# A streaming encoder step on one core: both out-projections as three rounded products

## What is computed

```python
def _mix_even(...):
    ...
    out = jnp.concatenate([o_a.reshape(bsz, L, A_W), o_b], axis=-1) @ w_out   # (L, 1024) @ (1024, 1024)

def _mix_odd(...):
    ...
    o = _rmsnorm(o.astype(h.dtype), norm_g) * jax.nn.silu(z.reshape(bsz, L, C_HEADS, C_HEAD_DIM))
    out = o.reshape(bsz, L, C_W) @ w_out

def _trunk(x, past, prm):
    for i in range(DEPTH):
        x = x + 0.5 * _swiglu(rmsnorm(x), ...)       # feed-forward, 1024 -> 2816 -> 1024
        x = x + mixed                                # even or odd mixer
        x = x + 0.5 * _swiglu(rmsnorm(x), ...)
```

## Time and profile before

| | |
|---|---|
| median of 3 runs | 1662.07 us (1659.82 to 1662.42) |
| profiled execution, its span | 1662.3 us |
| mean granted TensorE clock | 0.947 |
| TensorE busy | 1514.3 us (91%) |
| VectorE busy | 917.8 us (55%) |
| ScalarE busy | 587.6 us (35%) |
| GpSimd busy | 314.9 us (19%) |

### The profile page before, as it was taken

One profiled execution on the slowest core, in us unless ns is written; L12 is line 12 of the kernel. 1 busy time (PEld: TensorE's weight loads), 2 busy tenths in 40 slices (PEclk: granted clock), 3 DMA queues, 4 the chain that ended last, 5 costly groups with the idle time before them and its releaser, 6 DMA issues.

```text
span 1662.3 us, 25537 instructions
## 1 busy us (share of the span) xinstructions
PE 1514.3 (91%) x9878; PEld 1450.1 (87%) x9878; DVE 917.8 (55%) x1511; ACT 587.6 (35%) x881; POOL 314.9 (19%) x319
## 2 busy tenths in 40 slices
PE   7699998997779999999999998798869889999997
PEld 6699997996757999999999996698868776999997
DVE  3466554278542666555666543868864341666642
ACT  5233333446331433334333323354422321533321
POOL 2000023755004000021000123344334002000000
PEclk9899998999879999999999998798979899999999
DMA  8755850434103555952557722323300002455651
GB/s 203 151 151 151 214 149 25 127 107 149 38 1 94 140 147 150 232 135 76 153 151 191 195 69 55 94 84 102 106 22 1 1 19 85 126 147 147 169 162 40
DMA packets 323804, 189.52 MB, mean 114 GB/s; under 512 B 11146, under 2 KB 320902, under 8 KB 323734
## 3 DMA queue, kind: packets, MB, share of 16 engines
q1 hardware_dynamic: 321088, 181.95, 40.0%
q0 software_dynamic: 2064, 6.58, 1.9%
q10 hardware_dynamic: 588, 0.12, 0.0%
HBM read 183.22 MB, written 5.40 MB: 113 GB/s over the span
## 4 chain that ended last, share of the span: by engine, by line
PE 82%; DVE 10%; ACT 4%; issue 2%; DMA 1%; SPq 1%; POOL 0%; ACTq 0%; DVEq 0%; POOLq 0%
PE PS L560 18%; PE PS L561 18%; PE PS L562 18%; PE PS L610 4%; PE PS L626 3%; PE PS L627 3%; PE PS L628 3%; DVE RA L1920 2%; PE PS L1035 1%; PE PS L1018 1%; PE PS L1030 1%; DMA gu<-in_ffn_w_up 1%; DVE RB L1931 1%; PE PS L1108 1%; PE PS L972 1%
## 5 line engine op out<-in xcount | busy, mean ns | idle before, releaser
L560 PE MATMUL PS<-h_hi,w_parts 128*128 128x320 f32 x1408 | 440.9, 313 | 27.0 <-DVE w_parts L1596 15.5
L561 PE MATMUL PS<-h_lo,w_parts 128*128 128x320 f32 x1408 | 438.6, 311 | 0.0
L562 PE MATMUL PS<-h_hi,w_parts 128*128 128x320 f32 x1408 | 438.3, 311 | 0.0
L560 PEld LDWEIGHTS PS<-h_hi,w_parts 128*128 128x128 f32 x1408 | 267.6, 190 | 30.0 <-DVE w_parts L1596 16.0
L561 PEld LDWEIGHTS PS<-h_lo,w_parts 128*128 128x128 f32 x1408 | 267.6, 190 | 0.3
L562 PEld LDWEIGHTS PS<-h_hi,w_parts 128*128 128x128 f32 x1408 | 267.5, 190 | 0.0
L1169 ACT ACTIVATE w_parts<-gu 128x1024 fp32r<-128x1024 f32 x176 | 176.5, 1050 | 184.8 <-PE PS L562 154.3
L1596 DVE TENSOR_TENSOR w_parts<-gu,w_parts 128x1024 fp32r<-128x1024 f32 x176 | 207.9, 1223 | 44.0 <-ACT w_parts L1169 43.8
L560 PE MATMUL PS<-act_hi,w_parts 128*128 128x320 f32 x704 | 217.5, 309 | 0.0
L561 PE MATMUL PS<-act_lo,w_parts 128*128 128x320 f32 x704 | 217.5, 309 | 0.0
L562 PE MATMUL PS<-act_hi,w_parts 128*128 128x320 f32 x704 | 217.5, 309 | 0.0
(11 more groups left out here) (336 smaller groups left out, 2078.5 us busy)
## 6 DMA issues: line engine op xcount, KB each, us to landing
gu<-in_ffn_w_gate SPq DMA_DIRECT2D x88, 512.0 KB, 4.0
gu<-in_ffn_w_up SPq DMA_DIRECT2D x88, 512.0 KB, 5.2
dn<-in_ffn_w_down SPq DMA_DIRECT2D x32, 1408.0 KB, 7.0
gu<-in_od_w_in SPq DMA_DIRECT2D x32, 512.0 KB, 5.0
gu<-in_ev_w_in SPq DMA_DIRECT2D x26, 512.0 KB, 4.8
dn<-in_ev_w_out SPq DMA_DIRECT2D x4, 1024.0 KB, 5.5
dn<-in_od_w_out SPq DMA_DIRECT2D x4, 1024.0 KB, 5.4
bias_rows<-RB POOLq DMA_DIRECT2D x1, 1280.0 KB, 28.6
```

What stands on the lines that cost most here:

```text
L560: mm(out, w_hi, hi, start=first, stop=False)
L561: mm(out, w_hi, lo, start=False, stop=False)
L562: return mm(out, w_lo, hi, start=False, stop=last)
```

## The change

Both out-projections become three products. The output of the mixers is kept in two parts, ev_o_hi and ev_o_lo (od_o_hi, od_o_lo), the weights in tiles wo of two parts, 256 columns wide, two buffers for each layer.

- TensorE: project_out does 24 matmuls for each output tile instead of 8. It waits for the remainders of the weight tile (wo_lo) and the output's remainders. In the even layer it begins with k = 4 to 7 (the gated heads), which need o_lo 1, and waits for the attention heads (pv_evac) only at the fifth k.
- ScalarE: heads_high rounds the heads' output from PSUM, out_high the odd chunks', split_out the weights, in two halves of 128x1024. The rounding of tiles 2 and 3 waits for dn_done of the output tile that frees their buffer. In the even layer these stand behind the split of the next feed-forward's first weights; in the odd layer tile 2 stands ahead of it and tile 3 behind.
- VectorE: heads_low and out_low subtract instead of copying; split_out does the remainder of even tile 1 ahead of the feed-forward's split, and of tiles 2 and 3 ahead of residuals 2 and 4.
- GpSimd: the remainders of even tile 0 and of odd tiles 0 and 1.
- Loads: a slot of dn is free when its tile's remainder has been taken (wo_lo), not when the products are done. The csr rows and some semaphores move; their work is the same.

Hunks that only merge semaphores or move csr are left out here.

```diff
@@ -312,6 +312,13 @@
+        ev_o_hi = rounded("ev_o_hi", RB_at, KT, T)
+        ev_o_lo = rounded("ev_o_lo", RB_at + T_QB * T, KT, T)
+        ev_wo = (rounded("ev_wo0", RB_at + bd_at + 320, 2, 2048), rounded("ev_wo1", RA_at, 2, 2048))
+        od_o_hi = rounded("od_o_hi", RA_at + 2560, KT, T)
+        od_o_lo = rounded("od_o_lo", hT_at, KT, T)
+        od_wo = (rounded("od_wo0", RB_at + 5120, 2, 2048), rounded("od_wo1", RB_at + dm_at, 2, 2048))
+
         def product_bank(c):
@@ -418,7 +426,9 @@
                     return lo_done, halves_before(f, FT + n - DN_FFN[f] + 1)
-            return dn_done, n + 1
+            if n < DN_EV + 4:
+                return wo_lo, 2 * (n - DN_EV + 1)
+            return wo_lo, 8 + 2 * (n - DN_OD + 1)
@@ -600,15 +610,24 @@
-            def project_out(base_dn, base_x):
+            def project_out(base_dn, base_x, wo, lo_before, out_hi, out_lo, first):
                 for m in range(KT):
 ...
                     if m % 2 == 0:
-                        pe.wait_ge(dn_loaded[n % 2], 16 * (n // 2 + 1))
+                        pe.wait_ge(wo_lo, lo_before + 2 * (m // 2 + 1))
                     pe.wait_ge(x_upd, base_x + 1 + m)
-                    for k in range(KT):
-                        ins = mm(bank(4 + m % 2, T), dn[:, n % 2, k * 256 + (m % 2) * P:k * 256 + (m % 2) * P + P],
-                                 oT[:, k, :], start=(k == 0), stop=(k == KT - 1))
+                    out = bank(4 + m % 2, T)
+                    for i in range(KT):
+                        k = (first + i) % KT
+                        at = k * 256 + (m % 2) * P
+                        w_hi, w_lo = (wo[m // 2 % 2][:, part, at:at + P] for part in range(2))
+                        if m == 0 and base_dn == DN_EV and i == 0:
+                            pe.wait_ge(o_lo, 1)
+                        if m == 0 and base_dn == DN_EV and i == 4:
+                            pe.wait_ge(s["pv_evac"], NCH)
+                        mm(out, w_hi, out_hi[:, k, :], start=(i == 0), stop=False)
+                        mm(out, w_hi, out_lo[:, k, :], start=False, stop=False)
+                        ins = mm(out, w_lo, out_hi[:, k, :], start=False, stop=(i == KT - 1))
                     ins.then_inc((dn_half, dn_done)[m % 2], 1)
@@ -664,9 +683,9 @@
                 attention()
-                pe.wait_ge(s["ob_ready"], 4)
-                pe.wait_ge(s["pv_evac"], 5)
-                project_out(DN_EV, X_EV)
+                pe.wait_ge(s["l_done"], 8)
+                pe.wait_ge(s["pt_evac"], 8)
+                project_out(DN_EV, X_EV, ev_wo, 0, ev_o_hi, ev_o_lo, 4)
@@ -914,12 +933,12 @@
                 recurrence()
-                pe.wait_ge(o["og"], NCH)
-                project_out(DN_OD, X_OD)
+                pe.wait_ge(o_lo, 1 + NCH)
+                project_out(DN_OD, X_OD, od_wo, 8, od_o_hi, od_o_lo, 0)
 ...
-                pe.wait_ge(o["ab_in"], 48)
+                pe.wait_ge(small_in, 96)
                 for k in range(KT):
@@ -1293,6 +1312,16 @@
                     split_gate_up(2, 0, 0, 0)
+
+            def split_out(base_dn, m, wo):
+
+                n = base_dn + m
+                sc.wait_ge(dn_loaded[n % 2], 16 * (n // 2 + 1))
+                if m >= 2:
+                    sc.wait_ge(dn_done, n - 1)
+                for half in range(2):
+                    w = slice(half * 1024, (half + 1) * 1024)
+                    copy(wo[m % 2][:, 0, w], dn[:, n % 2, w]).then_inc(wo_hi, 1)
@@ -1401,23 +1430,41 @@
+                def heads_high(b):
+                    sc.wait_ge(s["pv_pe"], b + 1)
+                    for par in range(2):
+                        h = slice(par * A_D, (par + 1) * A_D)
+                        ins = copy(ev_o_hi[h, 0:4, b * CH:(b + 1) * CH],
+                                   bank((6, 7, 6, 7, 7)[b])[h, :].rearrange("p (a c) -> p a c", a=4)
+                                   [:, :, par * CH:(par + 1) * CH])
+                    ins.then_inc(o_hi, 1)
+
                 exps(0)
 ...
                 turned(1)
+                sc.wait_ge(out_sem, 16 * 8)
+                copy(ev_o_hi[:, 4:8, :], oT[:, 4:8, :]).then_inc(o_hi, 1)
                 turned(2)
+                heads_high(0)
+                heads_high(1)
                 exps(3)
                 turned(3)
+                heads_high(2)
                 exps_sample(0)
                 exps_sample(1)
+                heads_high(3)
                 turned_sample(0)
 ...
                 exps_sample(3)
+                split_out(DN_EV, 0, ev_wo)
                 turned_sample(2)
                 turned_sample(3)
+                heads_high(4)
+                split_out(DN_EV, 1, ev_wo)
@@ -1517,6 +1564,12 @@
+                def out_high(n_):
+
+                    w = slice(CHUNK_ORDER[n_] * CH, (CHUNK_ORDER[n_] + 1) * CH)
+                    sc.wait_ge(o["og"], n_ + 1)
+                    copy(od_o_hi[:, :, w], oT[:, :, w]).then_inc(o_hi, 1)
+
                 for n_, c in enumerate(CHUNK_ORDER):
@@ -1531,10 +1584,19 @@
                     act_(sqO, bank(2), ACT.Square).then_inc(o["osq"], 1)
+                    if n_ > 1:
+                        out_high(n_ - 2)
+                    if n_ == 2:
+                        sc.wait_ge(o["zt"], 2)
+                        split_out(DN_OD, 0, od_wo)
+                    if n_ == 3:
+                        split_out(DN_OD, 1, od_wo)
+                out_high(NCH - 2)
                 root_out(NCH - 1)
 ...
                 copy(csr[0:6, 2048:3072], PS[0:6, 3072:4096]).then_inc(o["cs_evac"], 1)
+                out_high(NCH - 1)
@@ -1549,6 +1611,8 @@
             split_gate_up(1, 0, 0, 0)
+            split_out(DN_EV, 2, ev_wo)
+            split_out(DN_EV, 3, ev_wo)
             ffn(1, C_FFN + 8, X_FFN[1])
@@ -1556,7 +1620,9 @@
             odd()
+            split_out(DN_OD, 2, od_wo)
             split_gate_up(3, 0, 0, 0)
+            split_out(DN_OD, 3, od_wo)
             ffn(3, C_FFN + 24, X_FFN[3])
@@ -1652,8 +1718,19 @@
-            def residual(base_dn):
+            def split_out(base_dn, m, wo, before):
+
+                for half in range(2):
+                    w = slice(half * 1024, (half + 1) * 1024)
+                    ve.wait_ge(wo_lo, before + 2 * m + half)
+                    ve.wait_ge(wo_hi, before + 2 * m + half + 1)
+                    tt(wo[m % 2][:, 1, w], dn[:, (base_dn + m) % 2, w], wo[m % 2][:, 0, w].bitcast(F32), ALU.subtract)\
+                        .then_inc(wo_lo, 1)
+
+            def residual(base_dn, wo, before):
                 for m in range(KT):
+                    if m in (2, 4):
+                        split_out(base_dn, m // 2 + 1, wo, before)
                     ve.wait_ge((dn_half, dn_done)[m % 2], half_count(base_dn, m))
@@ -1853,13 +1930,13 @@
-                def heads_out(b):
-                    ve.wait_ge(s["pv_pe"], b + 1)
+                def heads_low(b):
+                    ve.wait_ge(o_hi, b + 2)
                     for par in range(2):
                         h = slice(par * A_D, (par + 1) * A_D)
-                        ins = cp(oT[h, 0:4, b * CH:(b + 1) * CH],
-                                 bank((6, 7, 6, 7, 7)[b])[h, :].rearrange("p (a c) -> p a c", a=4)
-                                 [:, :, par * CH:(par + 1) * CH])
+                        w = slice(b * CH, (b + 1) * CH)
+                        ins = tt(ev_o_lo[h, 0:4, w], bank((6, 7, 6, 7, 7)[b])[h, :].rearrange("p (a c) -> p a c", a=4)
+                                 [:, :, par * CH:(par + 1) * CH], ev_o_hi[h, 0:4, w].bitcast(F32), ALU.subtract)
                     ins.then_inc(s["pv_evac"], 1)
@@ -1871,22 +1948,25 @@
                 logits(3)
-                heads_out(0)
-                heads_out(1)
+                ve.wait_ge(o_hi, 1)
+                tt(ev_o_lo[:, 4:8, :], oT[:, 4:8, :], ev_o_hi[:, 4:8, :].bitcast(F32), ALU.subtract).then_inc(o_lo, 1)
+                heads_low(0)
+                heads_low(1)
                 probs(3)
-                heads_out(2)
-                heads_out(3)
+                heads_low(2)
                 logits_sample(0)
                 logits_sample(1)
+                heads_low(3)
                 probs_sample(0)
 ...
                 probs_sample(3)
-                heads_out(4)
+                heads_low(4)
+                split_out(DN_EV, 1, ev_wo, 0)
                 split(1, gu, 0, 0, 0)
-                residual(DN_EV)
+                residual(DN_EV, ev_wo, 0)
@@ -2040,6 +2120,12 @@
+                def out_low(n_):
+
+                    w = slice(CHUNK_ORDER[n_] * CH, (CHUNK_ORDER[n_] + 1) * CH)
+                    ve.wait_ge(o_hi, NCH + 1 + n_ + 1)
+                    tt(od_o_lo[:, :, w], oT[:, :, w], od_o_hi[:, :, w].bitcast(F32), ALU.subtract).then_inc(o_lo, 1)
+
                 ve.wait_ge(o["states"], 1)
@@ -2061,13 +2147,19 @@
                         ve.wait_ge(o["zt"], 1)
-                        link(stt(zth, zth, 1.0, zT, ALU.add, ALU.mult))
```

(28 more changed lines are left out.)

15 lines of the change are left out of this document (8 added, 7 removed).

## The result

The changed kernel took 1665.63 us (median of 7 runs, 1664.32 to 1669.19) where the kernel before, in the same comparison, took 1661.4 us (7 runs, 1659.27 to 1664.2): a ratio of 1.0032, 95% interval 1.0021 to 1.0043. The forecast was 2.2 us slower, the measurement says 5.3 us slower (3.5 to 7.1). Measured twice more, beside the experiments, the changed kernel stood at 1.0007 (0.9998 to 1.0016) and 1.0015 (1.0004 to 1.0025). The three intervals do not all overlap, so comparisons of one and the same pair differ by more than their intervals say. The two later ones ran on different chips, and which chip the first had is not on record, so whether the chip makes the difference is open. Weighted by their intervals, the three give 1.0016, or 2.7 us. It is a small loss, and its size is known to about 2 us.

The account below looks back on a forecast made before the run. TensorE, busy 91% of the span, was taken to bound the kernel. Even layer +3.7 - 6.3 = -2.6 us and odd layer +2.5 - 6.3 + 6.0 + 2.6 = +4.8 gave +2.2: 1664.3 us, range 1659.5 to 1668.5.

Parts of the forecast that it names:

- Products: Both out-projections: 64 matmuls of 0.54 us become 192 of 0.147 us, 34.5 against 28.2 us, gaining 6.3 us each.
- Even start: Even out-projection starts at 497.4 rather than 493.72 us, 3.7 us later (3.2 to 4.3 by the bounds).
- (a): Even layer's attention: values of block 2 wait for the release of block 0's bank and start 1.6 us later.
- (b): Even layer's attention: first sample probabilities come 2.65 us later, behind block 3's rounding on ScalarE and subtraction on VectorE.
- (c): Even weight tile 0: ScalarE's rounding costs TensorE 0.25 us; GpSimd's two subtractions of 2.5 us end at 497.35.
- Odd layer ahead of the projection: Recurrence and its tail before the odd out-projection: +0.7 and +1.8 us, together a start 2.5 us later.
- The recurrence: Odd layer: ScalarE's added rounding and weight tile, 2.63 us against 2.27 idle, delay two chunks 0.36 us each, +0.7 us.
- The stall: Odd out-projection: after block 1, TensorE idles 6.0 us until VectorE adds tile 0's residual behind the feed-forward weights' split.
- The clock: Two new 1.2 GHz stretches, at the odd projection's start and behind its stall, +1.3 us each; bounds 0 and 4.5 for both.
- The clock held low for 7 us: Rival: odd projection's first two blocks run wholly at 0.50, costing 5.8 rather than 1.3 us; 1668.5 us, chance 0.15.
- GpSimd slowed by half: Rival: GpSimd's two subtractions take half as long again, even start 2.5 us later; about 1667 us, chance 0.10.
- attention absorbs (a) and (b): Level rival: late release is covered, even projection starts about 493.4, even layer gives 6.6 us; 1660.3 us, chance 0.15.

Follow-up runs that it names:

- warm products: Changed kernel with both reorderings (odd layer's weight roundings, heads' roundings) plus five unread float32 matmuls ahead of the odd projection; 1654.76 us, ratio 0.9954 to the kernel before.
- the odd layer alone: Only the odd out-projection in three products, the even one as in the kernel before; 1665.16 us, ratio 1.0017 to the kernel before.
- the kernel with the longer stall: Changed kernel with two more ScalarE copies of 128x1024 ahead of rounding the next feed-forward's first weights; 1669.82 us, ratio 1.0045 to the kernel before.
- both edits: Changed kernel with odd tile 2 rounded behind the feed-forward split, and heads' roundings moved earlier on ScalarE; together 1654.18 and 1653.98 us, ratios 0.9962 and 0.9949.
- the heads' order: Changed kernel with ScalarE rounding blocks 0 and 1 before block 2's transposed copies, block 3 before the first sample exponential; 1660.98 us, ratio 0.9998 to before.

## Why the forecast came out as it did

**The sign and the size.** The forecast of 1664.3 us stood on a median of 1662.07 for the kernel before, so it said +2.2 us. The first comparison gives +5.3, all three together +2.7. Sign and mechanism were right. That the size came so near is in part luck: in the profile the clock cost more than I took and the products gave less, together 1.5 us, while the even start, the odd lead-in and feed-forward 3 took 2.3 us less than I took or counted. That the first comparison fell beyond 0.2% and the other two within it cannot be put down to a step of the sum.

**Products: right in kind, 0.1 to 0.6 us too large.** Matmuls start 0.147 us apart (13 intervals from 1384.05 to 1385.96 us in the changed kernel), an undisturbed projection takes 28.1 us (the one with warm products), against 28.2 forecast. The even one takes 28.2 to 28.5 us; 0.3 us of that is block 2's wait for the residual of tile 0, which the prediction had just in time. The step from 34.3 is -5.7 to -6.2 us where I took -6.3. The prediction's other estimate, 8.6 us, would have been much too large; the rows decided rightly.

**Even start: +3.7 forecast, +3.0 in the first profile.** (a) was 1.6 us: the wait went from 1.16 to 2.81, 1.65 us. (b) was 2.65 us: the idle time before the first sample turn went from 5.85 to 8.51, 2.66 us (the prediction's three terms add up to 482.41, not 482.45, which changes nothing). (c) was the term with a gap in it. GpSimd took 2.33 us for a half, not 2.5; and before the change, 1.0 us of idle stood between the last values and the projection, which the change does away with, since the projection no longer waits there for the last heads' output. I had used that gap without naming it. That GpSimd would be the last event holds in five of eight executions. Over these eight, the time from the end of block 2's turn to the projection is 37.3 to 39.1 us, 38.1 on average, against 35.2 in the kernel before and 35.7 in the odd layer alone, whose even side is that of before: 2.4 to 2.9 us longer. Its spread goes with the clock in the attention's thin work, which I had held fixed.

**Odd layer ahead of the projection: +2.5 forecast, +2.2 measured, from other parts.** The tail was 1.8 us; from the first conv transpose to the projection it is 8.2 instead of 6.6 us, +1.6. The recurrence was +0.7 and is not there: from its start to the conv transposes it took 62.5 us before and 62.2 to 62.6 us in every kernel with the change. The step that failed is the delay of 0.36 us for each of two chunks. It summed the rounding and the weight tile to 2.63 us against 2.27 of idle, and copies that follow each other overlap by about 0.1 us each: in the changed kernel ScalarE starts the rounding at 1344.05 and the copy of the new values at 1346.46, 2.41 us later. The rest of the 2.2 us, some 0.5 us, lies in the projection into the odd mixer, which the change doesn't touch and where executions differ by more. From the end of that projection to the out-projection it is 178.1 us in the two kernels with the odd layer of before and 179.7 to 179.9 us in all the others, so the change itself costs 1.7 us here. The term was right in sum by luck.

**The stall: 6.0 forecast, 5.99 measured.** It is there in every profile that keeps the change's order on ScalarE and VectorE at this place, gone when ScalarE's order is put back, down to one wait of 1.35 us when VectorE's is changed, and 7.88 when the chain is made 1.9 us longer. This is shown, not argued. It came from counting a queue's order, with durations of rows of before, from the one event that the chain newly hangs on, the end of block 1.

**The clock: 2.6 us forecast, 2.1 net.** Both slow stretches came where I put them in the changed kernel's profiles, each 12 or so matmuls 0.267 us apart instead of 0.147. They cost more than the 1.3 us taken for each: 1.5 us the first (29.7 against 28.1 us with the warm products) and 1.9 us the second (37.5 less 29.7 less the 6.0 of the stall). The step that failed is that I counted only those that were new. The slow stretch that feed-forward 3 had before, 1.3 us, is gone in the three profiles of the changed kernel and in that of the odd layer alone. In the others it is there, also in the kernel with the longer stall, which has both of its own, so a simple rule that slow stretches exclude each other doesn't hold. Nor does the premise that the idle time ahead of the projection decides: 3.21 us brought a slow stretch in nine profiles and none in the tenth. What decides is open.

**The rivals.** The clock held low for 7 us did not happen: it rose again after 3.2 to 3.6 us, in three profiles after 5.2 to 5.4 us behind the stall. (By its own terms that rival came to 1668.8 us, 1664.3 + 5.8 - 1.3, not 1668.5.) GpSimd slowed by half did not happen either, at 2.33 us a half. That attention absorbs (a) and (b) is refuted by the two waits. None of the rivals said what the experiments found to be worth most, that one line's place in ScalarE's program turns the loss into a gain; the last sentence of the prediction names only VectorE's side of it.

## What to carry to other kernels

When a step gets a new input that exists only after the engine's own work (here tile 2 after block 1), follow every instruction behind it in that engine's program, and behind those on the engines they feed, back to the first engine: here three queues closed into a ring that cost 6 us. Put the work that waits for nothing new first; both edits that did so kept the gain of the products (9 to 11 us in all against the change as it was made). And do not book a clock stretch by one place: in these profiles, where one went, the next was often longer or came where none was, once without any edit nearby, so count them over the whole neighbourhood and over more than one execution.

## What the runs showed of the hardware

**Slow stretches move.** With the same gap ahead of feed-forward 3 and the same work, its first 6 us were granted 0.72 before and 1.00 in the changed kernel. TensorE's 40 us before differ: no slow stretch there in the one, two in the other. That this is the cause is not shown. With the heads' order, the odd layer has the same program and the same 3.21 us of idle as in the changed kernel, and its first 7 us were granted 1.00, while the changed kernel had 0.50 from 1379.0 to 1382.2.

**Three rounded products for one in float32.** At 320 columns and full clock they cost 28.1 / 34.3 = 0.82 of it: 0.147 us for a rounded product, 0.54 us for a float32 one.

**VectorE and GpSimd slow each other.** VectorE's two subtractions of 128x1024 took 2.36 us at 1389.49 us, with GpSimd idle, and 3.23 us three microseconds later, while GpSimd worked on 128x320. GpSimd's additions of 128x320 (line 2230) took 0.86 us at best and 1.74 in the middle in the changed kernel; the best ones lie where VectorE is idle, those of 1.7 us and more beside its subtractions. Its squares (lines 2229 and 2232) mostly took 0.72 us, 1.58 us here. The changed kernel's timeline and line 2230:

```profile
1393.13 1.58 POOL L2229 TENSOR_TENSOR RB<-xT 128x320 f32<-128x320 f32 x1
1394.79 1.73 POOL L2230 TENSOR_TENSOR RB<-RB 128x320 f32<-128x320 f32 x1
...
1392.57 3.23 DVE L1727 TENSOR_TENSOR od_wo<-dn,od_wo 128x1024 fp32r<-128x1024 f32 x2
...
L2230 POOL TENSOR_TENSOR RB<-RB x35: 857/1741/2142, 215.2 to 1416.9; 128x320 f32<-128x320 f32 x35
```

The Trainium skill (GPSIMD Engine Reference, section Specifications) names VectorE instructions with two SBUF inputs as those that GpSimd contends with; these rows agree, and show that VectorE pays as well, by a third. Here nobody waited for either.
